# RWKV state in 64x64 quarters: updating and reading a block-diagonal recurrent state a head at a time

## What is computed

```python
def step(S, inp):
    r_t, w_t, k_t, v_t, kk_t, a_t = inp
    s_kk = jnp.einsum('bhvk,bhk->bhv', S, kk_t)
    S = (S * w_t[:, :, None, :] - s_kk[..., None] * (kk_t * a_t)[:, :, None, :]
         + v_t[..., None] * k_t[:, :, None, :])
    return S, jnp.einsum('bhvk,bhk->bhv', S, r_t)
```

## Time and profile before

| | us |
|---|---|
| median of 3 runs | 1808.53 |
| the 3 runs | 1807.63, 1808.53, 1811.20 |
| the profiled execution, its own time | 1812.38 |
| its span, first to last instruction | 1810.3 |
| TensorE busy | 1776.4 (98%) |
| VectorE busy | 1199.0 (66%) |
| ScalarE busy | 813.7 (45%) |
| mean granted TensorE clock | 0.993 |

### The profile page before, as it was taken

How to read it: one execution, slowest core, us unless ns; L and a number is a source line. 1 busy time by engine, 2 the same in 40 slices (tenths; PEclk the granted TensorE clock), 3 DMA queues, 4 the chain that set the end, 5 groups by cost and what they waited for, 6 DMA issues and landing times.

```text
span 1810.3 us, 31353 instructions
## 1 busy us (share of the span) xinstructions
PE 1776.4 (98%) x13186; PEld 1625.4 (90%) x13186; DVE 1199.0 (66%) x1727; ACT 813.7 (45%) x1081; POOL 19.4 (1%) x25
## 2 busy tenths in 40 slices
PE   9999999999999999999999999999999999999999
PEld 8889889788887788999988799999999997789999
DVE  3895455787887877877646468776886456445443
ACT  2326443534566765443444254434544335335342
POOL 0000000000000000000000000000000000000000
PEclk9999999999999999999999999999999999999999
DMA  8334420787898986887441058786687442034442
GB/s 322 140 113 167 150 83 1 291 323 292 337 358 336 353 342 249 312 328 302 166 161 49 24 221 322 318 315 258 251 314 281 186 140 72 25 140 186 164 186 70
DMA packets 65227, 391.45 MB, mean 216 GB/s; under 512 B 7360, under 2 KB 7488, under 8 KB 27328
## 3 DMA queue, kind: packets, MB, share of 16 engines
q1 hardware_dynamic: 64800, 389.38, 55.9%
q10 hardware_dynamic: 288, 0.08, 0.0%
HBM read 388.38 MB, written 1.05 MB: 215 GB/s over the span
## 4 chain that ended last, share of the span: by engine, by line
PE 89%; DVE 7%; ACT 2%; issue 1%; DMA 0%; POOL 0%; SPq 0%; DVEq 0%; ACTq 0%
PE bank L526 87%; PE bank L567 1%; DVE region L2258 1%; DVE slab_low L1939 1%; DMA slab<-in_w_up 0%; DVE region L2221 0%; DVE tiny L2220 0%; DVE xT L2051 0%; ACT w_hi L1478 0%; DVE region L2212 0%; DVE slab_low L2014 0%; DVE region L2545 0%; DVE d_low L1946 0%; ACT L1366 0%; ACT gate_hi L1495 0%
## 5 line engine op out<-in xcount | busy, mean ns | idle before, releaser
L1939 DVE TENSOR_TENSOR slab_low<-slab,w_hi 128x2048 fp32r<-128x2048 f32 x152 | 346.0, 2289 | 100.3 <-ACT w_hi L1478 99.7
L526 PE MATMUL bank<-h_hi,w_hi 128*128 128x256 f32 x1408 | 391.6, 281 | 0.0
L526 PE MATMUL bank<-h_hi,slab_low 128*128 128x256 f32 x1408 | 390.9, 281 | 0.0
L526 PE MATMUL bank<-h_lo,w_hi 128*128 128x256 f32 x1408 | 380.2, 281 | 0.0
L1478 ACT ACTIVATE w_hi<-slab 128x2048 fp32r<-128x2048 f32 x152 | 291.1, 1917 | 96.2 <-DMA slab<-in_w_ffn_in 76.2
L526 PEld LDWEIGHTS bank<-h_hi,slab_low 128*128 128x128 f32 x1408 | 269.5, 191 | 0.0
L526 PEld LDWEIGHTS bank<-h_hi,w_hi 128*128 128x128 f32 x1408 | 264.7, 188 | 0.4
L526 PEld LDWEIGHTS bank<-h_lo,w_hi 128*128 128x128 f32 x1408 | 257.6, 188 | 0.0
L526 PE MATMUL bank<-gT_hi,d_hi 128*128 128x256 f32 x832 | 234.0, 281 | 0.8 <-DVE gT_lo L2136 0.8
L526 PE MATMUL bank<-gT_lo,d_hi 128*128 128x256 f32 x832 | 233.7, 281 | 0.0
L526 PE MATMUL bank<-gT_hi,d_low 128*128 128x256 f32 x832 | 233.6, 281 | 0.0
(11 more groups left out here) (281 smaller groups left out, 2831.7 us busy)
## 6 DMA issues: line engine op xcount, KB each, us to landing
slab<-in_w_ffn_in SPq DMA_DIRECT2D x88, 1024.0 KB, 8.4
slab<-in_w_up SPq DMA_DIRECT2D x64, 1024.0 KB, 8.7
region<-in_w_ada SPq DMA_DIRECT2D x128, 512.0 KB, 6.6
region<-in_w_ffn_out SPq DMA_DIRECT2D x44, 1024.0 KB, 4.8
region<-in_w_down SPq DMA_DIRECT2D x32, 1024.0 KB, 4.9
slab<-in_w_in SPq DMA_DIRECT2D x23, 1024.0 KB, 4.8
slab<-in_w_mix_in SPq DMA_DIRECT2D x20, 1024.0 KB, 7.9
hT<-in_w_ada SPq DMA_DIRECT2D x16, 512.0 KB, 7.9
```

What stands on the lines that cost most here:

```text
L526: return nc.tensor.matmul(o, lhsT, rhs, start=start, stop=True, skip_group_check=True)
L1939: V_.tensor_tensor(slab_low[slot][:, :], slab[slot][:, :], w_hi[h % 3][:, :].bitcast(F), ALU.subtract)\
```

## The change

The state is handled in quarters of the array. Rho becomes four products of one head each: the head's 64x64 block as weights, its own 64 partitions of `rho`, its own 64 partitions of the output. The state update becomes eight products of 64x64 with 64 moving columns, each going to the partitions of its head, so that for each pair of heads one 64x128 strip holds the diagonal blocks alone. VectorE adds them to the state with two instructions of 64 partitions by 2x64 in place of one of 128x256; the multiplication by decay and mask is as it was. Two semaphores are new, both raised by TensorE and waited for by TensorE: `rho_done` ahead of the outputs from `vt`, and `y_part` (the chunk before has finished its outputs) ahead of rho from the second chunk on.

```diff
                         for c in range(2):
                             m = mm(ps[rows, c * P:(c + 1) * P], V["al"][:, c, tok], V["state"][:, c, :])
                         m.then_inc(S["for_act"], 1)
+                        if c4:
+                            pe.wait_ge(S["y_part"], w("y_part"))
                         for c in range(2):
-                            mm(bank[7][:, c * T + c4 * CHUNK:c * T + (c4 + 1) * CHUNK], V["state"][:, c, :],
-                               V["rho"][:, c, tok], c4 == 0 and c == 0)
+                            for heads in HALVES:
+                                m = mm(bank[7][heads, c * T + c4 * CHUNK:c * T + (c4 + 1) * CHUNK],
+                                       V["state"][heads, c, heads], V["rho"][heads, c, tok], c4 == 0 and c == 0)
+                        m.then_inc(S["rho_done"], 1)
                         short_half(4 + c4 // 2, c4 % 2)
...
+                        pe.wait_ge(S["rho_done"], w("rho_done"))
                         outputs("vt", "C2T")
                         pe.wait_ge(S["u_ready"], w("u_ready"))
                         if c4 < 3:
                             ps = product("dve")
-                            for c in range(2):
-                                mm(ps[:, c * P:(c + 1) * P], V["bt"][rows, t, c * P:(c + 1) * P],
-                                   V["negU"][rows, t, c * P:(c + 1) * P], c == 0)
-                                m = mm(ps[:, c * P:(c + 1) * P], V["kt"][rows, t, c * P:(c + 1) * P],
-                                       V["vt"][rows, t, c * P:(c + 1) * P])
+                            for x, (left, right) in enumerate((("kt", "vt"), ("bt", "negU"))):
+                                for h in range(4):
+                                    head = slice(h * CHUNK, (h + 1) * CHUNK)
+                                    m = mm(ps[HALVES[h % 2], (h // 2) * CHUNK:(h // 2 + 1) * CHUNK],
+                                           V[left][rows, t, head], V[right][rows, t, head], x == 0 and h < 2)
                             m.then_inc(S["for_dve"], 1)
                         turn(4 + c4)
                         m = outputs("negU", "C1T")
-                        if c4 == 3:
-                            m.then_inc(S["y_done"], 1)
+                        m.then_inc(S["y_done" if c4 == 3 else "y_part"], 1)
...
-                        read(V_.tensor_tensor(flat("state"), ps[:, 0:T], flat("state"), ALU.add))
+                        for heads in HALVES:
+                            own = V["state"][heads, :, heads]
+                            step(V_.tensor_tensor(own, ps[heads, 0:P].rearrange("p (a b) -> p a b", a=2), own,
+                                                  ALU.add))
+                        later()
+                        dve.sem_inc(S["read_by_dve"], 1)
+                        w("read_by_dve")
```

More of the change, by code:

```diff
@@ L156 @@
     "tt_ready": "the inverses of pairs", "u_ready": "a chunk's solution", "y_ready": "the output on chip", "y_mean": "its sums", "mix_ready": "RWKV output",
-    "conv_ready": "short convolution's output",
+    "conv_ready": "short convolution's output", "rho_done": "the state's part of a chunk's output",
+    "y_part": "the output of a chunk",
 }
```

## The result

| | before | with the change |
|---|---|---|
| median, runs | 1808.26 us, 8 | 1816.92 us, 8 |
| lowest and highest | 1806.98 to 1811.68 | 1810.58 to 1824.63 |
| ratio, 95% interval | | 1.0046, 1.0026 to 1.0065 |
| the profiled execution, its span | 1810.3 | 1808.5 |
| granted clock of the runs | 0.993 (profiled run) | 0.985 to 0.992 |

The change makes the kernel slower by 0.46%. The forecast was 1806.2 us, 0.13% faster, with a range of 1803.0 to 1809.6. The median lies 7 us above the range. The profile is a trap here: the execution that it recorded is the shortest of the eight, and its span is 1.8 us shorter than that of before. Even these 1.8 us are in part luck: its first loop starts at 989.45 us and that of before at 991.19, 1.7 us of lead from a stretch in which the two programs are the same.

A forecast was written before the change was run, and what follows sets the result against it. TensorE was taken to bound the kernel, busy 1776.4 of 1810.3 us. Updates (0.72) and rho (0.44) gave 1.16 us a layer, 2.3 in two layers, off the median 1808.53: 1806.2 us, range 1803.0 to 1809.6.

The forecast's parts named there:

- The price of the update: State update on TensorE: 0.61 us instead of 1.09, its own gain 0.48 us a chunk, in three chunks a layer.
- The new wait ahead of `turn`: Second and third chunk: `turn` waits 0.35 us for VectorE's `att_p`, leaving a gain of 0.12 us there.
- VectorE's sums: After the update: one sum of 0.42 us becomes two taking 0.6, 0.2 more, none of it on the path.
- The two new semaphores: `y_part` ahead of rho, `rho_done` ahead of the `vt` outputs: waits over when asked for, taken to cost nothing.
- The rival of quarters that take turns at a bank: Rho's quarters don't overlap: 0.61 us, a loss of 0.12 a chunk, 1808.0; chance 0.12, shared with costly waits.
- Rho: In each of four chunks a layer: 0.38 us instead of 0.49, gain 0.11 a chunk, 0.44 a layer.
- The sum: Both layers' gains: 0.72 us from updates plus 0.44 from rho, 1.16 a layer, 2.3 in two layers.
- the change of the clock: TensorE's granted clock in and behind the loops: the forecast time counted no gain or loss from it.
- The clock, against it: Second and third chunk: more waiting lets the clock fall within the loop, up to 3.4 us a layer, 1813.0; chance 0.08.

The follow-up runs named there:

- after_again: The changed kernel, unedited, measured a second time: 1817.60 us, ratio 1.0042 to the kernel before.
- before_idle: The kernel before, with one more VectorE instruction ahead of the probabilities in the second and third chunk, so that `att_p` comes later: 1820.02 us, ratio 1.0058.
- negu_first: The changed kernel with the outputs from `negU` moved ahead of `turn`: 1805.35 us, ratio 0.9982 to the kernel before.
- after_warm: The changed kernel with one unread product of 128x256 ahead of `turn` in the second and third chunk: 1807.26 us, ratio 0.9989 to the kernel before.

## Why the prediction was wrong

**What held.** TensorE bounds the loop and what follows it. The price of the update, 0.61 forecast and 0.62 measured, with sixteen records of two column quarters costing what eight in one quarter do. The new wait ahead of `turn`: forecast at 0.96 us from the update's start with 0.35 idle, measured 0.96 with 0.28. VectorE's sums: 0.6 and 0.61, hidden. The two new semaphores: nothing. The rival of quarters that take turns at a bank fell: rho took 0.38 us into one bank. The rule of the Trainium skill's page TensorEngine Tiling (Array Packing), section Restrictions and Gotchas, that tiles in different rows cannot access one PSUM bank at the same time, would have made it 0.61; the measurement decides against it, for tiles that also write different partitions.

**A term that was mis-sized.** Rho was to give 0.11 us a chunk and gave 0.07: the 0.49 that it took before was measured up to a filler whose form was rho's own. Now the filler comes behind a change of form and takes 0.05 longer. So the first loop gained 1.00 us, not 1.16. The second gained some 0.8, because its last wait was 0.19 us longer; no run says why. At full clock the runs of the changed kernel stand 2.1 to 2.9 us below those of before (1795.8 for the first eight, 1795.0 for after_again, 1797.9 before), with an error of about 0.5, where 2.3 had been forecast.

**The step that failed.** The sum put the change of the clock at nothing, and the runs put it at 11.7 us lost, against some 2 to 3 gained. The reason given for nothing is in the rivals. *The clock, against it* named the mechanism, the place and the waits, and was given 0.08. It was put aside with two arguments. The first was that the clock is 1.00 throughout the loop now, which told only that the loop of before is on the safe side, not by how much. The second was that TensorE loses 0.36 us more of a chunk, "not a whole us": the only wait known to be followed by a fall was the one of 1.43 us, and I took its size for the scale. before_idle shows that 0.22 us more in two chunks of a loop is enough. The price was too small as well: one fall a loop, 3.4 us each. In after_again's profile there are three falls within the loops, of 6.83, 10.24 and 10.24 us, besides those behind them. One fall does not use up the cause: in the second loop the third chunk's `turn` waited 0.28 us again after the first fall, and 1.3 us later the clock fell a second time.

There was a sign in what I had worked out: the sum said that the second and third chunk together would have 1.0 us less of TensorE's work (2 x 0.48) and be only 0.24 us shorter for it, since VectorE holds `turn`. When TensorE is relieved and the chunk doesn't shorten with it, its idle share grows: 0.33 us of 9.0 before, 0.6 of 8.8 after. The sum priced that idle time by what it did to the path alone.

**What stays open.** Why the clock falls in the loop in some executions and not in others of one kernel: the profiled executions of the change and of after_again have the same waits in the same places, and only the second has falls inside its loops. Only one execution of each kernel has a trace, so that the clock fell inside the loops in the other long runs too is inferred from their mean clocks, not seen. And how the 0.28 us ahead of `turn` and the 0.33 us ahead of the update share the cause was not separated: each cover took away one, or both.

## What to carry to other kernels

When an edit takes work off TensorE inside a latency-bound loop, ask what it does in the time it has won: if it waits, put work there in the same edit (a product from further down, half of a filler), since covering 0.28 us in four chunks was worth 10 to 12 us here. Where runs of one kernel scatter by 0.8% while a profile looks fine, compare the granted clock of all runs before any row of the trace, and multiply each span by its clock: what is left tells whether the instruction stream got shorter. A filler that stands in one piece ahead of one wait can often serve two.

## What the runs showed of the hardware

- A single wait of 0.28 us in each of two chunks of 8.8 us, beside one of 0.33 that was there, was followed by falls of TensorE's granted clock from 2.4 to 1.2 GHz for 6.83 or 10.24 us, in some executions. The whole-product kernel with 0.22 us more of waiting behaves the same way (before_idle, 1820.0 us); with the wait cut to 0.11 us the clock of the kernel before came back (negu_first, 0.995).
- A product that nobody reads, put in place of that wait, started the transposes 0.19 us later and made the kernel 10 us faster (after_warm).
- Products in the two diagonal quarters, and in two column quarters of the same rows, ran side by side into one PSUM bank: 0.38 us for eight records, 0.62 for sixteen, against 0.61 for eight in one quarter.
